# A hybrid SSD / retention / RWKV-7 decoder trunk with a routed mixture of experts: the routing of tokens to experts is rearranged

## The chip, the core and the metric

The kernel runs on one core of one Trainium2 chip. Its engines work side by side: TensorE (PE in the profile; PEld is its loading of the stationary operand), VectorE (DVE), ScalarE (ACT), GpSimd (POOL) and SyncE (SP, which here only starts transfers). The metric is the device time of the whole program in microseconds.

## The reference

Two layers over 512 tokens of width 1024, all float32. Layer 0 mixes tokens by SSD and retention with one output projection; layer 1 by RWKV-7 time mixing. Each layer ends in the mixture of experts that this change is about:

```
def hier_moe(h, wg, bg, we, be, w1, w3, w2):
    g_logits = t @ wg + bg                       # 4 groups
    g_prob = softmax(g_logits); g_idx = argmax(g_logits); g_gate = g_prob[g_idx]
    e_logits = (t @ we + be).reshape(-1, 4, 4)   # 16 experts
    top_v, top_i = top_k(e_logits[g_idx], 2)
    top_w = softmax(top_v) * g_gate
    combine = sum(one_hot(g_idx * 4 + top_i, 16) * top_w)
    for e in range(16):
        he = silu(t @ w1[e]) * (t @ w3[e])
        out = out + combine[:, e] * (he @ w2[e])
...
for layer in range(2):
    h = h + mix(rms_norm(h, norm_mix_w[layer]))
    h = h + hier_moe(rms_norm(h, norm_ffn_w[layer]), ...)
return rms_norm(h, norm_final_w)
```

## The kernel before

The program is a row of phases with a barrier between them. A phase is one block in which each engine has its own instruction stream; the streams meet by semaphores written out by hand (`wait_ge`, `then_inc`), and every engine works strictly in the order of its code. Nothing is scheduled by a planner, so what stands ahead of an instruction in its stream can hold it.

**Ahead of the experts.** Layer 0 ends its mixer in `proj_phase`, layer 1 in `rwkv_out_phase`. Both multiply by an output matrix, one tile of 128 tokens (m = 0 to 3) after another, add to the residual `t.h`, and run the RMSNorm `Norm` on it: `mean_square`, `root`, `inverse`, `scale` (into `xn`), `transposes` on TensorE into PSUM banks, `evacuate` into `ut`, the transposed tokens. `norm.store` writes `xn` to `token_rows` in HBM, from where tokens are gathered. In `rwkv_out_phase` the products of tile m use the banks 4 to 7, and so do the norm's transposes of tile m - 1.

**Routing.** `moe` starts with the logits (TensorE, in bands, then folded), the choice of group and two experts (`first_max`, three times, on VectorE), and counts: each token gets its rank in its expert's list by products with triangular and all-one matrices (`s_rank`). A list is cut into LARGE pieces of 96 slots and SMALL pieces of 64. VectorE works out which expert each visit serves (`listed`, written to `t.meta`, from where every engine reads it into a register by `expert` and `visits`) and at which slot it begins (`begins`).

**Visits.** The loop over visits treats two pieces at a time: A (96 tokens of expert e = 0's list, buffers `xa`) and B (64 tokens, `xb`). To find the tokens of a piece, VectorE compares the ranks with slot numbers (`equal_slots`), multiplies by token numbers (`times_ids`), sums (`sum_a`, `sum_b`); TensorE turns the result into a column (`turn_a`, `turn_b`); VectorE writes it as row numbers (`index_a`, `index_b`); GpSimd gathers the rows (`gather_b` one transfer, `gather_a` two); TensorE transposes them (`x_transposes`); VectorE evacuates (`x_evacuation`). Only then can the visit's products start (`s_xte`). A visit's products: with `w13` in four chunks j (release: `s_used`, `s_h`), SiLU and gating, transposes, then with `w2` in two chunks (release: `s_half`, `s_y`). SP loads the next visit's weights into each chunk as it is released: for two experts 8 transfers of 1 MB for `w13` and 4 for `w2`, 12.6 MB a visit.

Before the loop, the kernel gathers the tokens of visit 0 **and** of visit 1; inside visit i it finds and gathers those of visit i + 2, behind the first half of the `w2` products. SP loads the weights of expert 0 and then those of the first A piece at the start of `moe`, and waits for the whole table (`s_meta` at 3) before it enters its loop.

Of the kernel before, what the change touches and what calls it, by code (L numbers as in the profile page):

```python
# [21 lines left out]
P = 128  # L22
# [22 lines left out]
LARGE_UNITS = -(-(SEQ - SMALL) // LARGE)  # L45
# [6 lines left out]
ROUTER_ROWS = 32  # L52

# [25 lines left out]
def shape_constants():  # L79
# [9 lines left out]
    iota4 = np.tile(np.arange(4), (P, 1))  # L89
# [3 lines left out]
    more = np.tile((head[:, None] + LARGE * np.arange(LARGE_UNITS)[None, :] + SMALL).reshape(1, -1), (P, 1))  # L93
# [5 lines left out]
    common = np.concatenate([ident, upto, before, neg, same_half, half_sel, iota4, visit, np.ones((P, P)), fold, slot_of, row_of, iota16, np.tile(head, (P, 1)), more, expert_step, row_half], 1).astype(f)  # L99
# [17 lines left out]
C_IOTA = C_HALF + 2  # L117
C_VISIT = C_IOTA + 4
# [7 lines left out]
C_EXPERT_STEP = C_MORE + EXPERTS * LARGE_UNITS  # L126
C_ROWHALF = C_EXPERT_STEP + UNIT_LISTS
C_ALL = C_ROWHALF + STEPS
# [56 lines left out]

class Norm:
# [39 lines left out]
    def transposes(self, pe, m):  # L226
        t = self.t
        pe.wait_ge(self.s_xn, m + 1)
        if self.used[m] is not None:
            pe.wait_ge(self.s_ev, 2 * (self.used[m] + 1))  # L230
        for k in range(KD):
            mm = t.nc.tensor.transpose(t.bank[self.banks[m][k // 4]][:, (k % 4) * P:(k % 4 + 1) * P], self.xn[:, m, k * P:(k + 1) * P], t.ident)  # L232
            if k % 4 == 3:
                mm.then_inc(self.s_tr, 1)

# [87 lines left out]
def load_phase(t, a):  # L323

    nc = t.nc
    with ExitStack() as c:
# [13 lines left out]
        def _(act):  # L340
# [4 lines left out]
            act.dma_start(t.router[:, :, :, :], a["router"]).then_inc(t.s_more, 16)  # L345
# [8 lines left out]
def in_proj_phase(t, a, ut, xbc, xc, z, g, v, q, k, dt, bt, qr, kr, qt, kt, kd, tmp, a_dt, nacum, cum, ecum, ea):  # L354
# [26 lines left out]
    with ExitStack() as c:  # L381
# [23 lines left out]
        def _(pe):  # L405
            for i, (kind, n, m) in enumerate(steps):
# [464 lines left out]
def proj_phase(t, tag, srcs, scales, mt, chunks, ring, w_sem, ffn_layer):  # L871
# [5 lines left out]
    with ExitStack() as c:  # L877
# [11 lines left out]
        def _(sp):  # L889
            for n in range(2, len(chunks)):  # L890
# [5 lines left out]
                sp.dma_start(ring[n % 2], chunks[n]).then_inc(w_sem[n % 2], 16)  # L896
            norm.store(sp, ffn_layer)

        @block.tensor
        def _(pe):  # L900
# [7 lines left out]
            for n in range(len(chunks)):  # L908
                half, part = divmod(n, n_half)
                pe.wait_ge(w_sem[n % 2], 16 * (n // 2 + 1))  # L910
                for m in range(NT):
# [8 lines left out]
                    if n == len(chunks) - 1 and m:  # L920
                        norm.transposes(pe, m - 1)
            norm.transposes(pe, NT - 1)

# [12 lines left out]
        def _(dve):  # L936
            for half in range(2):
# [8 lines left out]
            for m in range(NT):  # L946
                norm.evacuate(dve, m)
# [13 lines left out]
def ffn_norm(t, c, layer, banks, used):  # L961

    A = views(t, AT_FFN, [("ut", (KD, SEQ)), ("xn", (NT, D))])
# [4 lines left out]
def moe(t, a, layer):  # L968

    nc = t.nc  # L970
    NL = GROUPS + EXPERTS
# [9 lines left out]
                     ("table", (2, TABLE, UNIT_LISTS))])  # L981
    ut, bank = A["ut"], t.bank
    w13, w2 = (a[n][layer] for n in ("moe_w13", "moe_w2"))
    w_col = t.col(f"ffn{layer}")
    with ExitStack() as c:
        sem = lambda n: t.semaphore(f"moe{layer}_{n}")
        s_part, s_lg, s_exp, s_route, s_pick, s_prefix, s_rank = (sem(n) for n in (
            "partial_logits", "logits", "exp", "route", "picked", "prefixes", "ranked"))
# [4 lines left out]
        s_w13 = [sem(f"w13_loaded{i}") for i in range(4)]  # L993
        s_w2 = [sem(f"w2_loaded{i}") for i in range(2)]
# [4 lines left out]
        taken = [AT_FFN + KD * SEQ + NT * D]  # L999
# [7 lines left out]
        wr = t.router[:, layer]  # L1007
        lg = sb("logits", [P, NT, NL])
        oh_g, cand_g = (sb(n, [P, NT, GROUPS]) for n in ("group", "cand_g"))
        sel, cand = (sb(n, [P, NT, EXPERTS]) for n in ("sel", "cand"))  # L1010
        mx = [sb(f"max{j}", [P, NT]) for j in range(3)]
        least, ex, den, gsum = (sb(n, [P, NT]) for n in ("least", "ex", "den", "gsum"))
# [3 lines left out]
        parts = sb("parts", [P, SEQ])  # L1016
        prod, over = (sb(n, [P, NT, EXPERTS]) for n in ("prod", "over"))
        in_head = sb("in_head", [P, NT])
        more = sb("more", [P, EXPERTS, LARGE_UNITS])
        units, begin, incl = (sb(n, [P, UNIT_LISTS]) for n in ("units", "begin", "incl"))  # L1020
# [8 lines left out]
        match_a, match_b = sb("match_a", [P, LARGE, NT]), sb("match_b", [P, SMALL, NT])  # L1029
        token_a, token_b = sb("token_a", [P, LARGE]), sb("token_b", [P, SMALL])  # L1030
        scaled = sb("scaled", [P, 2, TABLE, UNIT_LISTS])
# [17 lines left out]
        def _(sp):  # L1049
            for j in range(4):  # L1050
                sp.dma_start(b["w13"][:, 1, 2 * j:2 * j + 2], w13[0, j]).then_inc(s_w13[j], 16)
            for j in range(2):
                sp.dma_start(b["w2"][:, 1, 2 * j:2 * j + 2], w2[0, j]).then_inc(s_w2[j], 16)
            n = visits(sp)
            first = expert(sp, 0, 0)
            for j in range(4):
                sp.dma_start(b["w13"][:, 0, 2 * j:2 * j + 2], w13[bass.ds(first, 1), j].rearrange("o p k n -> p (o k) n")).then_inc(s_w13[j], 16)
            for j in range(2):
                sp.dma_start(b["w2"][:, 0, 2 * j:2 * j + 2], w2[bass.ds(first, 1), j].rearrange("o p k n -> p (o k) n")).then_inc(s_w2[j], 16)
            sp.wait_ge(s_meta, 3)  # L1060
# [21 lines left out]
        def _(pe):  # L1082
            quarters = P // ROUTER_ROWS
            for k in range(KD):
                r0 = k % quarters * ROUTER_ROWS
                mm = nc.tensor.matmul(bank[0][r0:r0 + ROUTER_ROWS, :], wr[:, k, :], ut[:, k, :],
                                      start=k < quarters, stop=k >= KD - quarters)
            mm.then_inc(s_part, 1)
            pe.wait_ge(s_part, 2)
            for m in range(NT):  # L1090
                mm = nc.tensor.matmul(bank[2][:, m * NL:(m + 1) * NL], parts[:, m * P:(m + 1) * P], t.common[:, C_FOLD:C_FOLD + NL],
# [1550 lines left out]
```

## Time and profile before

| what | value |
|---|---|
| median of 3 runs | 1708.24 us (1707.78 to 1712.01) |
| the profiled execution | 1702.24 us, its span 1700.4 us |
| TensorE busy | 1478.2 us, 87% of the span |
| VectorE / ScalarE / GpSimd busy | 37% / 22% / 11% |
| granted TensorE clock, mean | 0.94 of full |
| read from HBM / written | 304.64 MB / 27.26 MB |

The times of all rows below are counted from the start of the span. Layer 0's projection phase ends at 566.9, its loop over visits runs from 601.0 to about 853; layer 1's experts begin at 1377.2, their loop at 1411.6.

### The profile page before, as it was taken

To read this page: it belongs to the slowest core of one execution; us is meant where nothing else is said; L and a number is where in the kernel's file an instruction comes from. 1 tells how busy PE (TensorE), PEld (TensorE's weight loads), DVE (VectorE), ACT (ScalarE), POOL (GpSimd) and SP (SyncE) were. 2 spreads that over 40 slices of the span, in tenths; PEclk is the share of its full clock that TensorE was granted. 3 is DMA by queue.
4 is the path that set the end of the run, shared out by engine and by line. 5 is a ranking of instruction groups with operands and counts; after the bars stand their busy time and mean duration, and the time that the engine had idled before them with its cause. 6 is when DMAs were issued, how large, how long until landed. Compare 5 with 4: busy or idle time off the path is not lost. (4 is left out here: it accounts for less than half of the span.)

```text
span 1700.4 us, 26012 instructions
## 1 busy us (share of the span) xinstructions
PE 1478.2 (87%) x10560; PEld 759.3 (45%) x10560; DVE 623.5 (37%) x1271; ACT 375.6 (22%) x706; POOL 192.7 (11%) x211
## 2 busy tenths in 40 slices
PE   6999999979799489988929999989998858999891
PEld 3444444457444233333314444458996423343330
DVE  4421200048101542211247269455667244131124
ACT  1012111133200111111144067242232110111112
POOL 0000000016000010100020024110131001010002
PEclk9999999989899689999969999998999968999996
DMA  5424321020020699999852211000011059999995
GB/s 186 148 99 168 129 99 50 0 99 1 1 99 25 253 368 415 417 414 418 356 175 103 99 50 50 25 1 3 27 51 51 37 209 365 411 417 412 417 399 191
DMA packets 73060, 307.72 MB, mean 181 GB/s; under 512 B 7584, under 2 KB 9760, under 8 KB 48032
## 3 DMA queue, kind: packets, MB, share of 16 engines
q1 hardware_dynamic: 54736, 262.68, 39.1%
q0 software_dynamic: 9344, 31.99, 5.0%
q10 hardware_dynamic: 8912, 12.10, 2.0%
q8 instruction: 48, 0.79, 0.2%
q14 instruction: 20, 0.16, 0.0%
HBM read 304.64 MB, written 27.26 MB: 195 GB/s over the span
## 5 line engine op out<-in xcount | busy, mean ns | idle before, releaser
L1149 PE MATMUL bank<-arena 128*32 128x512 f32 x2048 | 241.2, 613 | 25.3 <-DMA arena<-in_moe_w 24.1
L446 PE MATMUL bank<-arena 128*128 128x512 f32 x512 | 222.1, 592 | 0.0
L1569 PE MATMUL bank<-arena 128*128 128x512 f32 (+1 forms) x448 | 192.7, 601 | 1.4 <-ACT arena L1672 1.4
L446 PEld LDWEIGHTS bank<-arena 128*128 128x128 f32 x512 | 96.3, 190 | 117.5 <-issue 117.5
L1434 DVE TENSOR_TENSOR arena<-arena,bank 64x512 f32<-64x512 f32 x32 | 22.1, 691 | 332.4 <-ACT arena L1215 332.4
L1465 POOL DMA_INDIRECT arena<-token_rows,index x60 | 56.9, 948 | 730.4 <-DVE index L1298 694.6
L1149 PEld LDWEIGHTS bank<-arena 128*32 128x32 f32 x2048 | 65.6, 113 | 164.1 <-issue 124.1
L1569 PEld LDWEIGHTS bank<-arena 128*128 128x128 f32 (+1 forms) x448 | 83.4, 191 | 103.0 <-issue 97.9
L1181 PE MATMUL bank<-arena 128*32 128x512 f32 x1024 | 116.5, 595 | 0.0
L913 PE MATMUL bank<-arena 128*128 128x512 f32 x256 | 110.5, 593 | 1.5 <-ACT arena L929 1.5
L443 PE MATMUL bank<-arena 128*128 128x512 f32 x192 | 82.6, 592 | 1.2 <-PEq L275 1.2
L913 PEld LDWEIGHTS bank<-arena 128*128 128x128 f32 x256 | 48.4, 190 | 61.5 <-issue 59.8
L1215 ACT ACTIVATE arena<-bank 64x512 f32<-64x512 f32 x32 | 18.8, 588 | 236.2 <-PE bank L1149 236.2
L1156 PE MATMUL bank<-arena 128*32 128x256 f32 x1024 | 66.9, 379 | 0.0
L2353 PE MATMUL bank<-arena 128*128 128x512 f32 x128 | 57.5, 609 | 5.4 <-DVE arena L239 5.4
L232 PE MATMUL bank<-common,arena 128*128 128x128 f32 x128 | 23.1, 349 | 43.9 <-ACT arena L218 40.0
L471 ACT ACTIVATE arena<-bank 128x512 f32<-128x512 f32 x32 | 19.1, 597 | 189.4 <-PE bank L446 189.4
L443 PEld LDWEIGHTS bank<-arena 128*128 128x128 f32 x192 | 36.4, 190 | 46.9 <-issue 45.4
L1181 PEld LDWEIGHTS bank<-arena 128*32 128x32 f32 x1024 | 30.0, 109 | 58.8 <-issue 57.4
L1156 PEld LDWEIGHTS bank<-arena 128*32 128x32 f32 x1024 | 32.9, 110 | 50.2 <-issue 39.0
L2225 DVE TENSOR_TENSOR arena<-bank,common 128x512 f32<-128x512 f32 x48 | 31.0, 687 | 60.6 <-PE bank L2008 60.5
L941 DVE TENSOR_TENSOR h<-h,bank 128x512 f32<-128x512 f32 x8 | 5.5, 688 | 114.0 <-PE bank L913 114.0
(373 smaller groups left out, 1916.4 us busy)
## 6 DMA issues: line engine op xcount, KB each, us to landing
arena<-in_moe_w SPq DMA_DIRECT2D x216, 1024.0 KB
arena<-in_w_in_e SPq DMA_DIRECT2D x11, 2048.0 KB, 9.1
slot_rows<-zero POOLq DMA_DIRECT2D x20, 512.0 KB, 7.9
arena<-in_w_out_e SPq DMA_DIRECT2D x4, 2048.0 KB, 8.6
slot_rows<-arena ACTq DMA_DIRECT2D x64, 128.0 KB, 8.1
token_rows<-arena SPq DMA_DIRECT2D x8, 512.0 KB, 2.6
arena<-in_rw_wr SPq DMA_DIRECT2D x2, 2048.0 KB, 12.9
arena<-in_rw_wk SPq DMA_DIRECT2D x2, 2048.0 KB, 7.9
```

The costliest lines, as they stand in the source:

```text
L232: mm = t.nc.tensor.transpose(t.bank[self.banks[m][k // 4]][:, (k % 4) * P:(k % 4 + 1) * P], self.xn[:, m, k * P:(k + 1) * P], t.ident)
L443: mm = nc.tensor.matmul(bank[:, :], w[:, kk, m * P:(m + 1) * P], ut[:, kk, :], start=kk == 0, stop=kk == KD - 1)
L446: mm = nc.tensor.matmul(bank[:, 0:width], ut[:, kk, m * P:(m + 1) * P], w[:, kk, 0:width], start=kk == 0, stop=kk == KD - 1)
L913: mm = nc.tensor.matmul(t.bank[4 * half + m][:, :], mt[:, part * KD + kk, m * P:(m + 1) * P], ring[n % 2][:, kk, :], start=part == 0 and k ...
L1149: mm = nc.tensor.matmul(bank[H[s]][band * BAND:(band + 1) * BAND, :], xt[:, kk, half, s * BAND:(s + 1) * BAND], b["w13"][:, e, k, w * FF:( ...
L1156: mm = nc.tensor.matmul(bank[H[2]][band * BAND:(band + 1) * BAND, 0:FF // 2], b["xta"][:, kk, half, SMALL:LARGE], b["w13"][:, 0, k, band * ...
L1181: mm = nc.tensor.matmul(bank[Y[s]][band * BAND:(band + 1) * BAND, :], b["ht"][:, k, s * PAIR + e * BAND:s * PAIR + (e + 1) * BAND], b["w2" ...
L1434: nc.vector.tensor_tensor(u, b["silu"][PAIR:P, s, :], bank[H[s]][PAIR:P, :], ALU.mult).then_inc(s_u, 1)
L1465: return nc.gpsimd.indirect_dma_start(out=x, out_offset=None, in_=halves, in_offset=bass.IndirectOffsetOnAxis(ap=t.index[0:n, at:at + 1], ...
L1569: mm = nc.tensor.matmul(t.bank[i % BANKS][0:rows, :], left, right, start=n == 0, stop=n == len(pairs) - 1)
L2225: nc.vector.tensor_tensor(four(u[name][rr]), four(t.bank[5 + (f + rr) % 3][:, :]), mask(col), ALU.mult).then_inc(s_sc_e, 1)
L2353: mm = nc.tensor.matmul(t.bank[4 + 2 * (m % 2) + half][:, :], mt[:, k_, m * P:(m + 1) * P], ring[half][:, k_, :], start=k_ == 0, stop=k_ = ...
```

## The change

1. **Logits.** Each `Norm.logits(m)` multiplies the tokens of a tile by the router's 20 columns (8 products) inside the phase ahead of `moe`, into bank 5. `proj_phase` evacuates each tile's transposes as it goes instead of all at the end.
2. **Loads of expert 0** (`FirstExpert.load`, six transfers of 1 MB) are issued by SP in the phase ahead, before `norm.store`: in `proj_phase` after the seventh product group, in `rwkv_out_phase` after the RWKV norm of the last tile.
3. **Choice by counting rivals.** The logits lie in a padded array with -3e38 around each group of four. Every logit is compared with its three rivals on the left (>=) and on the right (>); the sum is its place in the group. Place 0 is the first, place below 2 is among the two.
4. **New lists.** Large and small pieces of each expert are counted in one comparison of 192 elements. A visits beyond the large pieces take small pieces from the end of the list. The first A expert is worked out ahead of everything else and handed to SP alone (`s_meta` at 1).
5. **First rows by products.** The tokens of visit 0's A piece are no longer gathered: TensorE multiplies `xn` by the selection matrix `match_a` (`first_x`, two halves of 16 products).
6. **One gather less ahead.** Before the loop only visit 0 is prepared. Inside visit i the tokens of visit i + 1 are turned behind the first `w13` chunk, indexed, gathered, and transposed in the same visit.
7. **Softmax and expert weights** move on VectorE from the choice to behind the last evacuation before the loop. SP now waits for `s_meta` at 4 before its loop.
8. **RWKV's last norm in other banks.** In `rwkv_out_phase` the norm's transposes use the banks 0 to 3, and products of tile m wait for the residual add of tile m - 2 only.

```
+class FirstExpert:
+    def load(self, sp):
+        for j in range(4):
+            sp.dma_start(self.room13[:, 1, 2 * j:2 * j + 2], self.w13[0, j]).then_inc(self.s_w13[j], 16)
+        for j in range(2):
+            sp.dma_start(self.room2[:, 1, 2 * j:2 * j + 2], self.w2[0, j]).then_inc(self.s_w2[j], 16)
+    def logits(self, pe, layer, m):
+        pe.wait_ge(self.s_ev, 2 * m + 2)
+        for k in range(KD):
+            t.nc.tensor.matmul(t.bank[LOGITS][:, m * ROUTED:(m + 1) * ROUTED], self.ut[:, k, m * P:(m + 1) * P], t.router[:, layer, k, 0:ROUTED],
...
 # rwkv_out_phase, tensor
-                    pe.wait_ge(norm.s_ev, 2 * (m - 1))
+                    pe.wait_ge(s_add, 2 * (m - 1))
...
-                if m:
-                    norm.transposes(pe, m - 1)
                 if m + 2 < NT:
                     transposes(m + 2)
+                if m:
+                    pe.wait_ge(s_ev, 2 * min(m + 2, NT))
+                    norm.transposes(pe, m - 1)
...
 # moe, tensor: before the loop
+            pe.wait_ge(s_matched, 1)
+            first_x(0)
             pe.wait_ge(s_tokens_b, 1)
             turn_b()
+            first_x(1)
             pe.wait_ge(s_xb, 16)
             x_transposes(b["xb"], 1, P)
...
 # moe, tensor: in the loop
+                    if j == 0:
+                        pe.wait_ge(s_tokens_b, i + 2)
+                        turn_b()
+                        pe.wait_ge(s_tokens_a, i + 1)
+                        turn_a()
...
 # moe, vector: before the loop
+            ch.add(nc.vector.tensor_tensor(beats[:, :, :, 0:3], rivals(0), alone, ALU.is_ge))
+            ch.link(nc.vector.tensor_tensor(beats[:, :, :, 3:6], rivals(EPG), alone, ALU.is_gt))
+            ch.link(nc.vector.tensor_reduce(place[:, :, :].rearrange("p m e -> p (m e)"), beaten[:, :, :], AX.X, ALU.add))
...
+            dve.wait_ge(s_xt, 1)
+            x_evacuation(b["xtb"], 1, 0, P)
+            dve.wait_ge(s_meta, 3)
+            second = [expert(dve, e, 1) for e in range(2)]
...
             listed(2, TABLE)
             nc.vector.tensor_copy(meta_of[:, :, 2:TABLE], of_visit[0:1, :, 2:TABLE]).then_inc(s_meta, 1)
             begins(2, TABLE)
...
 # moe, vector: in the loop
                 both = [expert(dve, e, i + 2) for e in range(2)]
+                dve.wait_ge(s_turned_b, i + 2)
+                dve.wait_ge(s_xb, 16 * i + 16)
+                index_b()
+                dve.wait_ge(s_turned_a, i + 1)
+                index_a()
                 for s in range(2):
                     dve.wait_ge(s_silu, STEPS * i + s + 1)
```

TensorE's order around the end of layer 0's projection and the start of routing. Before (L913 output products, L232 the norm's transposes, L1086 and L1091 logits, L1097 to L1100 ranks, L1105 to L1114 turns, L1120 transposes of gathered rows):

```order
L913 MATMUL bank<-arena 128x512 x8
L232 MATMUL bank<-common,arena 128x128 x16
L877 UNCONDITIONAL_BRANCH
L1081 UNCONDITIONAL_BRANCH
L1086 MATMUL bank<-arena,router 32x512 x8
L1091 MATMUL bank<-common,arena 128x20 x4
L1097 MATMUL bank<-arena,common 128x64
L1099 MATMUL bank<-arena,common 128x48
L1100 MATMUL bank<-arena,common 128x16
```

In the changed kernel (L941 products, L251 transposes, L259 logits, L1120 to L1124 ranks, L1151 `first_x`, L1129 `turn_b`, L1144 transposes of `xb`):

```order
L941 MATMUL bank<-arena 128x512 x8
L251 MATMUL bank<-common,arena 128x128 x8
L259 MATMUL bank<-narrow,arena 128x20 x16
L251 MATMUL bank<-common,arena 128x128 x8
L259 MATMUL bank<-narrow,arena 128x20 x16
L903 UNCONDITIONAL_BRANCH
L1116 UNCONDITIONAL_BRANCH
L1120 MATMUL bank<-arena,common 128x64
...
L1151 MATMUL bank<-arena 128x96 x16
L1129 MATMUL bank<-common,arena 64x1 x2
L1151 MATMUL bank<-arena 128x96 x16
L1144 MATMUL bank<-common,arena 128x128 x4
```

The logits moved ahead of the phase's end, 16 products among the last transposes and 16 behind them, and 32 products of 96 columns stand between the ranks and the loop.

VectorE's order at the entry of the loop over visits. Before (L1425 is the last weight of the experts, L1041 and L1046 load registers, L1434 and L1436 the gating, L1302 evacuates transposed rows; the indices follow at the end of the visit):

```order
L1425 TENSOR_TENSOR weight<-weight,arena 128x4
L1041 TENSOR_LOAD meta
L1041 ISA x2
L1429 UNCONDITIONAL_BRANCH
L1429 ISA
...
L1434 TENSOR_TENSOR arena<-arena,bank 64x512
...
L1436 TENSOR_TENSOR arena<-arena,bank 64x256
```

In the changed kernel (L1452 is that last weight; L1318 and L1314 are `index_b` and `index_a`; L1466 and L1468 the gating):

```order
L1452 TENSOR_TENSOR weight<-weight,arena 128x4
L1079 TENSOR_LOAD meta
L1079 ISA x2
L1456 UNCONDITIONAL_BRANCH
...
L1318 TENSOR_TENSOR index<-bank,common 128x1
L1461 REGISTER_ALU
L1314 TENSOR_TENSOR index<-bank,common 128x1
L1314 TENSOR_TENSOR index<-bank,common 64x1
...
L1466 TENSOR_TENSOR arena<-arena,bank 64x512
```

The row numbers of visit 1 are now written after the whole table, the slots and the weights of the experts, and ahead of visit 0's gating; before, both pieces of visit 1 were indexed ahead of the table.

## Rows read from the trace of the kernel before

**Rows 1.** Page, costliest groups: line, engine, tiles xcount | busy, mean ns | idle, releaser

```profile
L1149 PE MATMUL bank<-arena 128*32 128x512 f32 x2048 | 241.2, 613 | 25.3 <-DMA arena<-in_moe_w 24.1
```

**Rows 2.** Windows: stretch, engines' busy us (instructions), granted clock, DMA share, GB/s

```profile
600.00:605.00 5.00, 4.40 (x24) 1.25 (x27) 4.90 (x7) 0.00 (x0) 2.82 (x3) 0.51 1.01 413
...
720.00:740.00 20.00, 17.37 (x192) 5.90 (x188) 0.69 (x1) 2.64 (x4) 0.34 (x1) 1.00 1.02 412
```

**Rows 3.** Timeline of TensorE in layer 0's loop: start, us, line [idle <-releaser]

```profile
601.01 5.53 PE L1149 MATMUL bank<-arena 128*32 128x512 f32 x32 [0.60 <-DVE arena L1302]
...
632.20 3.62 PE L1149 MATMUL bank<-arena 128*32 128x512 f32 x32
...
661.47 3.62 PE L1149 MATMUL bank<-arena 128*32 128x512 f32 x32
...
763.82 3.64 PE L1149 MATMUL bank<-arena 128*32 128x512 f32 x32 [2.71 <-DMA arena<-in_moe_w]
```

**Rows 4.** Timeline of SP's weight loads, both layers

```profile
607.89 13.65 SPq L1070 DMA_DIRECT2D arena<-in_moe_w  x8
...
627.64 5.97 SPq L1078 DMA_DIRECT2D arena<-in_moe_w  x4
...
1419.35 13.66 SPq L1070 DMA_DIRECT2D arena<-in_moe_w  x8
```

**Rows 5.** Timeline, end of layer 0's projection and routing, and layer 1's logits

```profile
551.89 7.03 PE L913 MATMUL bank<-arena 128*128 128x512 f32 x16
...
571.31 1.07 PE L1091 MATMUL bank<-common,arena 128*128 128x20 f32 x8 [0.71 <-ACT arena L1203]
...
572.42 0.24 DVE L1249 TENSOR_TENSOR arena<-bank,rows 128x80 f32<-128x80 f32 x1 [5.33 <-PE bank L1091]
...
579.52 0.27 DVE L1323 SCALAR_TENSOR_TENSOR arena<-bank,arena 128x64 f32<-128x64 f32 x1 [1.13 <-PE bank L1100]
...
1381.62 1.89 PE L1091 MATMUL bank<-common,arena 128*128 128x20 f32 x8 [0.71 <-ACT arena L1203]
```

**Rows 6.** Timeline of the gathers before layer 0's loop

```profile
584.86 1.02 POOL L1465 DMA_INDIRECT arena<-token_rows,index  x1 [163.40 <-DVE index L1298]
...
590.99 1.19 POOL L1465 DMA_INDIRECT arena<-token_rows,index  x1 [0.30 <-issue]
...
591.53 1.11 PE L1120 MATMUL bank<-common,arena 128*128 128x128 f32 x4 [2.60 <-DMA arena<-token_rows,index]
...
598.68 1.73 PE L1120 MATMUL bank<-common,arena 128*128 128x128 f32 x8 [5.30 <-DMA arena<-token_rows,index]
```

**Rows 7.** The gathers' source line L1465: time from issue to landing

```profile
DMA to landing us min/median/max: 3.2/8.0/9.6
```

**Rows 8.** Timeline of VectorE and TensorE in layer 0's visit 0

```profile
600.79 1.25 DVE L1310 TENSOR_TENSOR arena<-arena 128x1056 f32<-128x1056 f32 x1
...
604.66 0.17 DVE L1392 CAST meta<-arena 1x32 int32<-1x32 f32 x1
...
612.74 0.17 DVE L1425 TENSOR_TENSOR weight<-weight,arena 128x4 f32<-128x4 f32 x1
...
622.85 3.64 PE L1181 MATMUL bank<-arena 128*32 128x512 f32 x32
...
623.54 0.35 DVE L1444 TENSOR_SCALAR arena<-arena 128x4 f32 x2
...
626.25 0.41 DVE L1290 TENSOR_REDUCE arena<-arena 128x64 f32<-128x256 f32 x1
```

**Rows 9.** Source line L1046: loading a register on VectorE, ns min/median/max

```profile
L1046 DVEq TENSOR_LOAD <-meta x38: 300/307/547, 585.2 to 1628.1; - x38
...
L1046 DVEq FUSED_REGOPS  x54: 71/190/216, 585.8 to 1628.5; - x54
```

**Rows 10.** Timeline of TensorE at the end of rwkv_out_phase

```profile
1337.72 15.67 PE L2353 MATMUL bank<-arena 128*128 128x512 f32 x32 [2.39 <-DVE arena L239]
...
1357.24 13.97 PE L2353 MATMUL bank<-arena 128*128 128x512 f32 x32 [2.98 <-DVE arena L239]
```

More of the change, by code:

```diff
@@ L98, in shape_constants @@
     fold = np.tile(np.eye(ROUTER_ROWS, GROUPS + EXPERTS), (P // ROUTER_ROWS, 1))
-    common = np.concatenate([ident, upto, before, neg, same_half, half_sel, iota4, visit, np.ones((P, P)), fold, slot_of, row_of, iota16, np.tile(head, (P, 1)), more, expert_step, row_half], 1).astype(f)
+    common = np.concatenate([ident, upto, before, neg, same_half, half_sel, visit, np.ones((P, P)), fold, slot_of, row_of, iota16, np.tile(head, (P, 1)), more, expert_step, row_half, -2 * visit - 1], 1).astype(f)
     lg = np.log(1.0 - 2.0 ** (-5.0 - np.arange(R_HEADS)))
@@ L921, in _ @@
                         norm.transposes(pe, m - 1)
+            norm.logits(pe, ffn_layer, 0)
+            norm.logits(pe, ffn_layer, 1)
             norm.transposes(pe, NT - 1)
+            norm.logits(pe, ffn_layer, 2)
+            norm.logits(pe, ffn_layer, 3)
         @block.scalar
@@ L945, in _ @@
                         norm.inverse(dve, m)
[L946 to L947 removed]
+                        if m:
+                            norm.evacuate(dve, m - 1)
+            norm.evacuate(dve, NT - 1)
 def first_max(nc, chain, onehot, x, mx, least, cand, iota):
@@ L1005, in sb @@
             return v
[L1007 to L1010, printed above, removed]
+        lists = ROUTED // EPG
+        beaten = sb("beaten", [P, NT * lists * EPG, 6])
+        place = sb("place", [P, NT, lists * EPG])
+        oh_g = sb("group", [P, NT, GROUPS])
         mx = [sb(f"max{j}", [P, NT]) for j in range(3)]
-        least, ex, den, gsum = (sb(n, [P, NT]) for n in ("least", "ex", "den", "gsum"))
+        ex, den, gsum = (sb(n, [P, NT]) for n in ("ex", "den", "gsum"))
         gexp = sb("gexp", [P, NT, GROUPS])
@@ L1082, in _ @@
         def _(pe):
[L1083 to L1091, printed above, removed]
-                                      start=True, stop=True)
-            mm.then_inc(s_lg, 1)
             flat = lambda ap: ap.rearrange("p m e -> p (m e)")
@@ L2311, in _, with rwkv_out_phase @@
             normed.squares(pool, 2)
-def rwkv_out_phase(t, a, y, v, g, lnw, lnb, sq, mt, ring, s_w, keep):
+def rwkv_out_phase(t, a, y, v, g, lnw, lnb, sq, mt, ring, s_w, keep, first):
     nc = t.nc
@@ L2326, in _ @@
         def _(sp):
+            sp.wait_ge(normed.s_y, 1)
+            first.load(sp)
             norm.store(sp, 1)
@@ L2443, in rwkv @@
     rwkv_scan_phase(t, a, M["sigma"], M["ag"], M["r"], M["k"], V["v"], V["g"], btok, ktok, u, state, keep, wo_ring, s_w)
-    rwkv_out_phase(t, a, btok, V["v"], V["g"], u["lnw"], u["lnb"], u["sq"], M["r"], wo_ring, s_w, keep)
+    first = FirstExpert(t, a, 1)
+    rwkv_out_phase(t, a, btok, V["v"], V["g"], u["lnw"], u["lnb"], u["sq"], M["r"], wo_ring, s_w, keep, first)
+    return first
 def final_phase(t, a, out, w, rows, y):
```

333 lines of the change are left out of this document (165 added, 168 removed).

## The prediction, made before the changed kernel was run

> **What bounds the kernel now.** I read the page's costliest groups first. They say who waits in the long loops over visits: TensorE's largest group idles 25.3 us in all, 24.1 of them for weights [rows 1]. The windows show why: in the middle of the loop the DMA share is 1.02 at 412 GB/s, TensorE is busy 17.37 of 20 us [rows 2]. Two paces stand against each other. Visits 1 and 2 start 29.3 us apart with no wait (632.20 and 661.47) [rows 3]. A visit's 12.6 MB of weights, its gathers (0.66 MB) and its stores (0.64 MB) take 13.9 MB / 412 GB/s = 33.7 us. So TensorE lives on weights loaded ahead and starves once these are used up [rows 3]. From there each layer ends when SP's stream of loads ends: only what moves that stream, or tears a hole into it, moves the end. The chain of waits covers only the last 27 us and tells nothing about routing.
>
> Next I read SP's timeline. The stream starts at 607.89 in layer 0 and at 1419.35 in layer 1; layer 0's first `w2` loads follow at 627.64 [rows 4]. Eight `w13` loads are 8.4 MB = 20.4 us. With 1 us from issue to first bytes (my choice), the `w13` part flows until 629.3, so the `w2` loads were there in time and the stream has no hole. In layer 1 the same point is 1440.7.
>
> **The change part by part, layer 0.** *Start of routing.* The last products end at 558.9 (551.89 + 7.03) [rows 5]. Then TensorE has 8 transposes, 16 products of 20 columns for the logits of two tiles, 8 transposes, 16 + 16 products again. Two instructions a product, 8 in 1.07 us at full clock (0.134 each) [rows 5], transposes at the same: 1.1 + 4.3 + 1.1 + 4.3 = 10.8, and 0.35 for the barrier: the logits are there at 570.0, before at 572.42 [rows 5]. The evacuations hide under the logits of earlier tiles.
>
> *Choice, ranks.* Before: 7.1 us from logits to ranks (572.42 to 579.52) [rows 5]. Now seven VectorE steps: 80 elements 0.24, three of 240 at 0.41 as for 256 elements [rows 8], two of them overlapping, two small at 0.2, gaps of 0.04: 1.9. Three prefix adds and two products: 1.7. Ranks at 573.6. Nine short steps give the first A expert (2.2) and six more its selection matrix (1.7): 577.5.
>
> *`first_x`.* No row shows it. Each half is 16 products, 32 instructions, bound by loading 128 x 128 operands as the logits are: 0.134 each at full clock, 0.236 at the low one (8 in 1.89) [rows 5], so 4.3 to 7.6 us. TensorE has idled by then, and in this stage the clock stood at 0.51 (1.2 GHz) until TensorE had worked for some microseconds [rows 2]. I take 6.7 for the first half: 584.2. `turn_b` and `index_b` 0.6, GpSimd starts 0.9 later: 585.7, before 584.86 [rows 6]. The B gather landed 6.7 us after GpSimd's start (591.53 - 584.86) [rows 6]: 592.4. The second half of `first_x` ends by 592.2 even at the low clock, hidden by that gather; without this cover it would cost its 4.3 to 7.6. Transposes and evacuation take 1.8 (2.1 for two pieces, 598.68 to 600.79) [rows 6, 8]. Call this point E: 594.2, before 600.79. The loop starts 6.6 us earlier.
>
> The Trainium skill (TensorE: Matmul & The Clock Gate, "Part 1: The HAM clock gate") says that throttled is the default state and activity releases it; it speaks against moving row selection onto an idle TensorE, and the rows at 0.51 agree. By it alone both halves could run low, which would move E by 0.9 us.
>
> *What VectorE has to do after E.* Two register loads at 0.55 (0.307, plus 0.19 of register arithmetic) [rows 9]: 1.1. Finding visit 1's pieces: 3.1 (623.54 to 626.66) [rows 8]. The softmax part moved here, ten short steps: 1.9. The table up to its cast to integers: 4.0 (600.79 to 604.83) [rows 8]. The rest, slots and weights: 8.1 (to 612.91) [rows 8]. Loop entry with three register loads: 2.0. Together 20.2 us. Only then does VectorE write visit 1's row numbers, though the tokens were turned long before. Queued behind them are visit 0's gating and GpSimd's gathers.
>
> *Visit 0's hole.* GpSimd starts 0.9 after the index, its third transfer 2.5 later (0.95 to 1.19 each and 0.30 between), landing 7.7 after that as in 590.99 to 598.68 [rows 6]: E + 31.3. The last transposes and the `ht2` evacuation: 2.0. The first half of `w2` up to SP's issue: 4.8 (622.85 to 627.64) [rows 4, 8], and 1.5 more since TensorE idled over 5 us and restarts at the low clock. SP issues visit 1's `w2` at E + 39.6 = 633.8; bytes flow from 634.8. SP waits for the table too, so its `w13` loads start at E + 1.1 + 3.1 + 1.9 + 4.0 + 1.5 (entry) = 605.8 and flow until 627.2. So the stream has a hole of 7.6 us and resumes 5.5 us later than before (634.8 against 629.3). Visit 1 then starts near 638 where it was 632.20 [rows 3], still with enough loaded ahead. Traffic behind that point is the same seven gathers and stores. **Layer 0: +5.5.**
>
> A gather's landing decides here. The Trainium skill (DMA: Bandwidth & Descriptors, "Anatomy of one DMA — SWDGE (gpsimd) path") puts a transfer at a fixed 2 us plus its bytes over 436 GB/s, an estimate of 2.6 us for 0.26 MB; with it the hole would shrink by 5 us and E come 4 earlier. The median of this line is 8.0 [rows 7], with the DMA engines full of weights, and I keep 7.7.
>
> **Layer 1.** In `rwkv_out_phase` TensorE waited 2.39 and 2.98 us for the norm's evacuations of the shared banks, and after the first wait a tile's products took 15.67 instead of 13.97 [rows 10]. The other banks take all three away: 7.1 us. The products end at 1357.24 + 13.97 - 7.1 = 1364.1. From there the steps are those of layer 0 (E came 35.3 after the products' end): E = 1399.4, bytes of `w2` from 1399.4 + 40.6 = 1440.0, before 1440.7. **Layer 1: -0.7.**
>
> **The rest.** Expert 0's loads move 16 us forward in layer 0, more in layer 1, where the DMA engines are nearly idle: worth nothing, as weights were not what E waited for; `norm.store` waits some 3 us behind them on SP and its rows are needed only at 585.7. In each layer's last visit a useless gather of 0.66 MB (1.6 us of DMA) no longer competes with the last stores: -0.5 each, between 0 and -1.6. Inside later visits the gathers start after the first chunk and have 15 us before TensorE asks: nothing. Contiguous router columns, constants: nothing.
>
> **Sum.** +5.5 - 0.7 - 1.0 = +3.8 on the profiled 1702.24. The runs shown have a median 6.0 above it, so I forecast 1708.24 + 3.8 = 1712.0 us.
>
> **Rivals.**
> *Faster: the hole does not open.* Should rows of visit 1 arrive by E + 24 (the `w13` loads flow until E + 33), SP's start is what counts: E + 11.6, so 605.8 for 607.89 and 1411.0 for 1419.35: -2.1 and -8.3, with the tails -11.4, 1697. It needs gathers 7 us faster than [rows 6]; the least landing, 3.2, speaks for it, the median against. With half of that, about 1704. Chance 0.24. Were the skill's 2.6 us a gather right, the time would be about this rival's; with no landing of the trace below 3.2 I give that 0.03 of the 0.24.
> *Slower: gathers land late under a full SP queue.* Both gathers on the path at the longest landing, 9.6 [rows 7]: 2.9 on E and 1.9 on visit 0, 4.8 a layer, +9.6 more: 1721.6. From about 0.7 us over my price a layer it decides for slower. For it: visit 0's gather meets SP's backlog, the old ones before the loop met less. Chance 0.36.
> *No change that can be told:* the 6.6 us won before the loop are given back in the hole and layer 1's bank gain pays for the rest; my sum is there. Chance 0.40.
>
> **Range and chances.** Per layer `first_x` is open by -2.4 to +0.9, the two landings by -7 to +4.8 at their ends, the restart clock by 1.5, register loads by 1. Two layers together give about -11 to +9: 1701 to 1721, 1712 likeliest. What a measurement tells from no change is 0.3%, 5.1 us. Faster 0.24, within 0.40, slower 0.36.
>
> **What would show it.** Right: ranks near 573.6, `first_x` 4 to 8 us a half, the loop near 594 and 1399; VectorE's first index in the loop some 20 us later, TensorE idle ahead of visit 0's transposes for the gather, a dip of the DMA share around 627 to 634, the next visit near 638; no waits of TensorE on evacuations in `rwkv_out_phase`. Wrong: transposes of visit 0 without a wait, or DMA at 1.0 throughout.

## The result, and the profile after

The changed kernel took 1720.4 us (median of four runs, 1718.2 to 1723.1), the kernel before 1708.0 on the same chip: a ratio of 1.0076 with a 95% interval of 1.0064 to 1.0088. It is slower, by 0.8% or 12 us. I had forecast 1712.0 with a range of 1701 to 1721 and a chance of 0.36 for slower. The profiled execution spans 1717.4 us, 17.0 more than that of before; some 4 us of these 17 are, as argued below, not the change's.

The page's rows that answer to [rows 1] and [rows 10], line, engine, tiles and count | busy, mean ns | idle, releaser:

```profile
L1173 PE MATMUL bank<-arena 128*32 128x512 f32 x2048 | 243.0, 616 | 29.1 <-DMA arena<-in_moe_w 27.3
...
L2375 PE MATMUL bank<-arena 128*128 128x512 f32 x128 | 55.6, 592 | 0.0
```

TensorE's wait for weights grew by 3.2 us and the waits of the RWKV output phase are gone. The page can't say more; the stretch around routing can. Timeline of the changed kernel, TensorE and VectorE, end of layer 0's projection phase to visit 1:

```profile
560.17 4.00 PE L259 MATMUL bank<-narrow,arena 128*128 128x20 f32 x32
...
564.01 1.95 PE L251 MATMUL bank<-common,arena 128*128 128x128 f32 x8
...
565.75 6.85 PE L259 MATMUL bank<-narrow,arena 128*128 128x20 f32 x32
...
572.90 0.25 DVE L1278 TENSOR_TENSOR arena<-bank,rows 128x80 f32<-128x80 f32 x1 [6.21 <-PEq L903]
...
577.04 0.36 DVE L1343 TENSOR_TENSOR arena<-bank,common 128x192 f32<-128x192 f32 x1 [1.35 <-PE bank L1124]
...
598.51 6.47 PE L1173 MATMUL bank<-arena 128*32 128x512 f32 x32 [0.87 <-DVE arena L1322]
...
619.17 0.16 DVE L1318 TENSOR_TENSOR index<-bank,common 128x1 uint32<-128x1 f32 x1 [2.43 <-issue]
...
627.51 1.11 PE L1144 MATMUL bank<-common,arena 128*128 128x128 f32 x4 [5.87 <-DMA arena<-token_rows,index]
...
631.22 1.73 PE L1144 MATMUL bank<-common,arena 128*128 128x128 f32 x8 [2.60 <-DMA arena<-token_rows,index]
...
642.63 3.61 PE L1173 MATMUL bank<-arena 128*32 128x512 f32 x32
```

Read from the end. Visit 1 starts at 642.63 (before 632.20 [rows 3]). Before it TensorE waited 5.87 and 2.60 us for the gathers of visit 1's rows, whose row numbers VectorE wrote only at 619.17. The loop itself starts at 598.51, earlier than the 601.01 of [rows 3], but far less than the 6.6 us I had counted on. SP's loads (both layers) and the windows over the same stretch:

```profile
611.08 9.42 SPq L1105 DMA_DIRECT2D arena<-in_moe_w  x8
638.81 5.24 SPq L1113 DMA_DIRECT2D arena<-in_moe_w  x4
...
1428.99 8.72 SPq L1105 DMA_DIRECT2D arena<-in_moe_w  x8
1457.34 5.22 SPq L1113 DMA_DIRECT2D arena<-in_moe_w  x4
```

```profile
560.00:565.00 5.00, 5.00 (x41) 5.00 (x39) 2.77 (x6) 1.44 (x2) 0.00 (x0) 0.83 1.02 429
565.00:570.00 5.00, 5.00 (x26) 5.00 (x24) 1.38 (x2) 0.00 (x0) 0.00 (x0) 0.50 0.96 342
...
630.00:635.00 5.00, 3.78 (x22) 2.02 (x26) 2.56 (x7) 0.28 (x1) 0.00 (x0) 0.50 0.96 387
635.00:640.00 5.00, 5.00 (x60) 1.56 (x52) 1.96 (x4) 0.00 (x0) 0.00 (x0) 1.00 0.09 20
640.00:645.00 5.00, 5.00 (x60) 1.68 (x56) 0.00 (x0) 1.58 (x3) 0.00 (x0) 1.00 0.93 372
...
1160.00:1170.00 10.00, 8.22 (x95) 7.63 (x94) 1.29 (x2) 1.68 (x3) 0.00 (x0) 0.53 0.01 2
1170.00:1180.00 10.00, 10.00 (x85) 9.21 (x85) 3.44 (x5) 2.00 (x4) 0.00 (x0) 0.50 0.01 2
...
1450.00:1455.00 5.00, 5.00 (x31) 1.75 (x34) 4.51 (x10) 0.28 (x1) 0.00 (x0) 0.58 0.55 229
1455.00:1460.00 5.00, 5.00 (x60) 1.68 (x56) 0.00 (x0) 0.60 (x1) 0.00 (x0) 1.00 0.32 90
```

The DMA share of 0.09 at 635 to 640 is the hole in the stream of weights. By the prediction's sum the `w13` loads issued at 611.08 have flowed by 632.5 (20.4 us and 1 to the first bytes), and the `w2` loads issued at 638.81 bring bytes from 639.8: 7.3 us. That sum leaves out visit 1's gathers, 0.66 MB or 1.6 us of the same DMA engines; by the shares the engines themselves were idle for some 5 us (0.96, 0.09 and 0.93 in the three windows from 630). Layer 1 has the same hole, by the sum between 1450.4 and 1458.3, by the shares of 0.55 and 0.32 some 5.7 us idle.

Along the program the profiled execution falls behind like this: 10.4 us at layer 0's visit 1 and 11.2 at its end; 14.9 where the RWKV output phase starts; 8.7 at its last product; 17.5 at layer 1's visit 1; 17.0 at the end. The 3.7 us between the second and the third figure lie in code that the change leaves alone: the granted clock was 0.53 and 0.50 from 1160 to 1180. The kernel before had 0.77 and 1.00 there, and the same code had 0.50 and 0.84 in run 1 and 0.67 and 1.00 in run 3. The timed medians stand 12.4 apart, not 17.0. So I take this stretch for the spread of single executions. Without it layer 0 costs 11.2 us, the output phase gives 6.2 back, layer 1's routing costs 8.8 to its visit 1, and 0.5 come back to the end: 13.3 in all.

### The profile page after: what moved, and what is told of

It is laid out like the page before. It is cut to its first block and busy times, and to the rows that moved or that the text cites. A ratio compares the mean times of both kernels' runs of the same rounds, so it can differ in the third digit from the quotient of the medians.

```text
span 1717.4 us, 26254 instructions
## 1 busy us (share of the span) xinstructions
PE 1508.8 (88%) x10700; PEld 799.2 (47%) x10700; DVE 632.3 (37%) x1261; ACT 374.4 (22%) x704; POOL 182.0 (11%) x201
## 5 line engine op out<-in xcount | busy, mean ns | idle before, releaser
L1173 PE MATMUL bank<-arena 128*32 128x512 f32 x2048 | 243.0, 616 | 29.1 <-DMA arena<-in_moe_w 27.3
L1173 PEld LDWEIGHTS bank<-arena 128*32 128x32 f32 x2048 | 67.6, 113 | 163.2 <-issue 124.1
L1491 POOL DMA_INDIRECT arena<-token_rows,index x50 | 47.0, 939 | 701.1 <-DVE index L1314 442.2
L1210 PE MATMUL bank<-arena 128*32 128x512 f32 x1024 | 118.6, 604 | 0.0
L941 PE MATMUL bank<-arena 128*128 128x512 f32 x256 | 110.5, 593 | 1.7 <-ACT arena L961 1.7
L1466 DVE TENSOR_TENSOR arena<-arena,bank 64x512 f32<-64x512 f32 x32 | 22.1, 690 | 201.6 <-ACT arena L1237 201.5
L941 PEld LDWEIGHTS bank<-arena 128*128 128x128 f32 x256 | 48.4, 190 | 61.8 <-issue 59.8
L1210 PEld LDWEIGHTS bank<-arena 128*32 128x32 f32 x1024 | 31.8, 111 | 63.7 <-issue 59.7
L1180 PEld LDWEIGHTS bank<-arena 128*32 128x32 f32 x1024 | 34.6, 110 | 48.3 <-issue 38.0
L1318 DVE TENSOR_TENSOR index<-bank,common 128x1 uint32<-128x1 f32 x18 | 2.9, 159 | 146.2 <-PE bank L1129 141.4
L251 PE MATMUL bank<-common,arena 128*128 128x128 f32 x128 | 22.8, 346 | 37.0 <-ACT arena L237 37.0
```

What stands on the lines that cost most here:

```text
L941: mm = nc.tensor.matmul(t.bank[4 * half + m][:, :], mt[:, part * KD + kk, m * P:(m + 1) * P], ring[n % 2][:, kk, :], start=part == 0 and k ...
L1173: mm = nc.tensor.matmul(bank[H[s]][band * BAND:(band + 1) * BAND, :], xt[:, kk, half, s * BAND:(s + 1) * BAND], b["w13"][:, e, k, w * FF:( ...
L1180: mm = nc.tensor.matmul(bank[H[2]][band * BAND:(band + 1) * BAND, 0:FF // 2], b["xta"][:, kk, half, SMALL:LARGE], b["w13"][:, 0, k, band * ...
L1210: mm = nc.tensor.matmul(bank[Y[s]][band * BAND:(band + 1) * BAND, :], b["ht"][:, k, s * PAIR + e * BAND:s * PAIR + (e + 1) * BAND], b["w2" ...
L1466: nc.vector.tensor_tensor(u, b["silu"][PAIR:P, s, :], bank[H[s]][PAIR:P, :], ALU.mult).then_inc(s_u, 1)
L1491: return nc.gpsimd.indirect_dma_start(out=x, out_offset=None, in_=halves, in_offset=bass.IndirectOffsetOnAxis(ap=t.index[0:n, at:at + 1], ...
```

## The experiments

Ratios are to the kernel before on the same chip; differences between two kernels are those of the ratios times 1708 us. My theory, **the hole**: visit 1's row numbers stand behind the table, slots and weights on VectorE, hence late gathers, late `w2`, and idle DMA. Rivals: SP's later start, gathers held up by the full DMA queue, the low clock.

### 1. Row numbers early

```
             nc.vector.tensor_copy(meta_of[:, :, 2:TABLE], ...).then_inc(s_meta, 1)
+            dve.wait_ge(s_turned_b, 2); dve.wait_ge(s_xb, 16); index_b()
+            dve.wait_ge(s_turned_a, 1); index_a()
...
-                (the same five lines at the head of the loop's body)
+                (at its end, for visit i + 2; TensorE turns once more behind the loop)
```

> The changed kernel, but VectorE writes visit 1's row numbers as soon as the table's cast is out (near 608.7 us in layer 0) and no longer behind slots and weights (619.17); in the loop it writes each next visit's numbers at the end of the body. Theory of the hole: GpSimd starts near 609.7, the third gather's issue is near 612.3 and lands 8.6 us later, near 621, about when TensorE gets there; w2 starts near 625, SP issues visit 1's w2 near 629.5, ahead of 632.5 where its w13 loads (issued from 611.08) have flowed. The dips of the DMA share near 635 to 640 in layer 0 and 1450 to 1459 in layer 1 vanish: -7.3 and -7.9 us, so 1705 us where the changed kernel has 1720.4. Rival, SP's late start (611.08 for 607.89) is what costs: no change, 1720. Rival, gathers meet the full DMA queue: half the gain, 1713.

Measured: 1703.3 us, ratio 0.9984 (0.9973 to 0.9995): 15.7 us below the changed kernel. GpSimd and TensorE in layer 0:

```profile
611.57 0.91 POOL L1500 DMA_INDIRECT arena<-token_rows,index  x1 [0.30 <-issue]
...
619.81 0.65 PE L1190 MATMUL bank<-common,arena 128*128 128x128 f32 x4 [1.60 <-DVE arena L1470]
620.30 1.43 PE L1144 MATMUL bank<-common,arena 128*128 128x128 f32 x12
...
630.40 3.62 PE L1173 MATMUL bank<-arena 128*32 128x512 f32 x32
```

The last gather is issued at 611.57, and the twelve transposes run at 620.30 without a wait. Visit 1 starts 12.2 us earlier. The edit moves the row numbers in later visits too, but there it changes nothing: the next gather starts 5.8 us behind the start of visit 1 in this kernel (636.20) and in the changed one (648.41). This one position in VectorE's order is worth more than all that the change costs.

### 2. SP starts early

```
-            sp.wait_ge(s_meta, 4)
+            sp.wait_ge(s_meta, 3)
             with sp.Fori(0, n) as i:
...
+                sp.wait_ge(s_meta, 4)          # last in the loop's body
```

> The changed kernel, but SP waits only for visit 1's experts ahead of its first loads of the loop, and for the rest of the table at the end of the loop's first pass; the w13 loads then start when TensorE is through its first chunk, near 607 for 611.08. Theory of the hole: the stream resumes where w2 is issued, and that hangs on the late row numbers; the hole only grows by what comes earlier: 1720 plus or minus 1.5 us. Rival, SP's start is what counts: -4 us a layer, 1712.

Measured: 1719.3 us, ratio 1.0080 (1.0063 to 1.0096), no change that can be told.

```profile
607.42 14.19 SPq L1105 DMA_DIRECT2D arena<-in_moe_w  x8
639.72 5.24 SPq L1113 DMA_DIRECT2D arena<-in_moe_w  x4
```

The stream started 3.7 us earlier and resumed no earlier: SP's start is not what costs while the hole is open. That rival falls.

### 3. Both

The two edits above, with the row numbers written even ahead of `listed(2, TABLE)`.

> Both edits, with visit 1's row numbers written even ahead of the long table. Theory of the hole: once rows are early the stream's start counts too: -7.6 and about -2.5 a layer, 1700 us, and faster than the kernel before (1708). Rival, only the row numbers count: as the first of these kernels, 1705. Rival, neither: 1720.

Measured: 1697.8 us, ratio 0.9958 (0.9945 to 0.9971): 20 us below the changed kernel, and below the kernel before. That is 4.4 us more than the first run. Two things differ from it, SP's start and the still earlier row numbers; in the first run the transposes already found their rows without a wait, while SP's loads start at 603.57 here for 610.16 there. So I put the gain down to SP's start, which counts once the hole is nearly shut. TensorE and the windows:

```profile
619.66 0.66 PE L1191 MATMUL bank<-common,arena 128*128 128x128 f32 x4 [3.15 <-DVE arena L1471]
```

```profile
625.00:630.00 5.00, 5.00 (x60) 1.60 (x56) 1.37 (x3) 0.47 (x1) 0.00 (x0) 1.00 0.74 252
```

What is late next is the gating of visit 0 (L1471), which stands behind slots and weights on VectorE; the share of 0.74 is what is left of the hole.

### 4. The banks alone

On the kernel before; the order of the two transposes is changed as in the diff ahead of the prediction:

```
-        norm = ffn_norm(t, c, 1, [(4 + 2 * (m % 2), 5 + 2 * (m % 2)) for m in range(NT)], (None,) * NT)
+        norm = ffn_norm(t, c, 1, [(2 * (m % 2), 1 + 2 * (m % 2)) for m in range(NT)], (None, None, 0, 1))
...
-                    pe.wait_ge(norm.s_ev, 2 * (m - 1))
+                    pe.wait_ge(s_add, 2 * (m - 1))
```

> The kernel before with only the RWKV norm's banks and the order around them changed. As I priced it: three waits gone, -7.1 us of 1708, so 1701. By the trace of the changed kernel (the phase took 61.8 us from its first transposes to its last product, before 67.8): -6.0, so 1702. Rival, the time is given back where layer 1's weights or routing wait anyway: 1708.

Measured: 1698.2 us, ratio 0.9964 (0.9949 to 0.9978), -6.1 us. Its products run without a wait and each tile at 13.90:

```profile
1338.96 13.90 PE L2353 MATMUL bank<-arena 128*128 128x512 f32 x32
...
1353.57 13.90 PE L2353 MATMUL bank<-arena 128*128 128x512 f32 x32
```

It isn't given back. If the two parts add up, routing as changed costs some 19 us, from which the banks take 6.

### 5. Logits among wide products

```
                     if n == len(chunks) - 1 and m:
                         norm.transposes(pe, m - 1)
+                    if n == len(chunks) - 1 and m >= 2:
+                        norm.logits(pe, ffn_layer, m - 2)
-            norm.logits(pe, ffn_layer, 0)
-            norm.logits(pe, ffn_layer, 1)
```

> The changed kernel, but in layer 0's projection phase the logits of tiles 0 and 1 stand between the wide products of tiles 2 and 3 and not behind the last of them. The work on TensorE is the same. Theory of the clock: the granted clock fell from 1.00 to 0.50 while TensorE was busy without a gap, behind 4 us of 20-column products; with half of them among wide products the transposes of tile 3 take 1.04 for 1.95 us and most of the last logits 0.125 each for 0.21: the choice starts 2 to 4 us earlier, and all of layer 0 with it: -3 of 1720.4, so 1717.4. Rival, the clock falls as early or the same time is lost elsewhere: 1720.

Measured: 1720.4 us, ratio 1.0066 (1.0050 to 1.0082), not told from the changed kernel; the expected 3 us aren't excluded by the times either. The trace decides:

```profile
563.22 1.86 PE L259 MATMUL bank<-narrow,arena 128*128 128x20 f32 x16
566.26 1.09 PE L251 MATMUL bank<-common,arena 128*128 128x128 f32 x8 [1.18 <-ACT arena L237]
567.19 6.21 PE L259 MATMUL bank<-narrow,arena 128*128 128x20 f32 x32
...
573.70 0.24 DVE L1278 TENSOR_TENSOR arena<-bank,rows 128x80 f32<-128x80 f32 x1 [5.46 <-PEq L903]
```

This execution was 1.25 us late before the edit could act (tile 1's transposes at 552.82 for 551.56), which has to be taken off. The transposes of tile 3 were at full clock, as I expected, but came 1.0 us later: the products of tile 3, and the norm that hangs on them, stood behind the moved logits. The last logits lost the clock all the same (6.21 for 6.85). The choice started at 573.70 for 572.90, so with the 1.25 taken off only 0.45 us earlier where I expected 2 to 4. The expectation was wrong: the last tile's norm is the chain here.

### 6. A dose

```
+            for _ in range(4):
+                ch.link(nc.vector.tensor_tensor(scaled[:, :, 2:TABLE, :], (itself), (itself), ALU.mult))
             dve.wait_ge(s_meta, 4)
             n = visits(dve)
```

> The changed kernel with four extra VectorE products of 1,056 elements (some 5.2 us) ahead of its loop, whose results nothing reads: a dose. Theory of the hole: visit 1's row numbers are 5.2 us later, TensorE waits as much longer, and since nothing else ends last there every us counts: +5.2 a layer, 1731. Rival, gathers are held up by the full DMA queue and land when the w13 loads let them: less than half, 1723. Rival, the hole costs nothing: 1720.

Measured: 1729.4 us, ratio 1.0124 (1.0107 to 1.0140), 8.2 us above the changed kernel. That is four fifths of the 10.4 added, and far from the rival's "less than half". In the traces visit 1 starts 4.6 us later in layer 0 (647.23 for 642.63), and layer 1's `w2` loads are issued 9.3 us later (1466.64 for 1457.34). The last gather took less time to TensorE's transposes than in the changed kernel, 7.8 us (626.92 to 634.69) and not 8.6 (622.66 to 631.22): some tenths of the dose are won back there.

### 7. Expert 0's loads late

```
             (first.load(sp) taken out of both preceding phases)
+            first.load(sp)
             sp.wait_ge(s_meta, 1)
             first_a = expert(sp, 0, 0)
```

> The changed kernel with expert 0's six loads back at the start of the routing phase, in both layers. As I priced their move: nothing, 1720 plus or minus 2. Rival: now they flow while the B gather is under way, which lands some us later (its 7.4 us from GpSimd's start to TensorE's transposes), and E with it: +2 to +4 a layer, 1724 to 1728. Rival: the token rows' stores no longer stand behind them on SP, a gain: 1718.

Measured: 1720.7 us, ratio 1.0070 (1.0057 to 1.0083). The loads were issued at 574.08 for 551.75, and the transposes of the B gather ran at 597.28 for 596.52, in an execution that was 1.1 us late before the edit could act; from GpSimd's start they took 7.0 us for 7.4. The early loads are worth nothing that can be measured, as I had priced them.

### 8. Slots and weights last

```
-            (slots and weights, from spare to t.weight[:, :, 1], ahead of the loop)
+            ch.wait()
             dve.wait_ge(s_meta, 4)
             n = visits(dve)
             with dve.Fori(0, n) as i:
...
+            (the same lines behind the loop)
```

> The kernel with both edits (early row numbers, SP's early start), and besides slots and weights moved from ahead of VectorE's loop to behind it. In the kernel with both edits TensorE waits 3.15 us for VectorE's gating of visit 0, which stands behind that block, and the DMA share still dips to 0.74 between 625 and 630. Theory: the wait goes, w2 starts near 619 for 622.5 and the dip closes: -3 a layer, 1692 where it had 1697.8. Rival: the dip was the gathers' and stays, 1697. Rival: the block behind the loop delays the combination: above 1698.

Measured: 1692.9 us, ratio 0.9907 (0.9893 to 0.9921): 16 us below the kernel before, 29 below the changed one. TensorE, VectorE and the windows:

```profile
619.15 0.66 PE L1191 MATMUL bank<-common,arena 128*128 128x128 f32 x4 [0.57 <-DVE arena L1440]
...
854.13 0.15 DVE L1466 TENSOR_SCALAR arena<-arena 128x1 f32<-128x1 f32 x1
...
859.26 0.16 DVE L1496 TENSOR_TENSOR weight<-weight,arena 128x4 f32<-128x4 f32 x1
...
866.40 1.28 DVE L292 SCALAR_TENSOR_TENSOR h<-arena,weight,h 128x1024 f32<-128x1024 f32 x1 [6.98 <-DMA arena<-slot_rows,slot]
```

```profile
625.00:630.00 5.00, 5.00 (x64) 1.95 (x60) 0.41 (x1) 1.21 (x3) 0.00 (x0) 1.00 1.01 419
```

That is 8.7 us below run 3 by the ratios, where 6 were expected. The wait of 3.15 is down to 0.57, the share is 1.01 where it was 0.74, and the 5.3 us of slots and weights hide behind the last visit.

### 9 to 12. TensorE kept busy

```
+            def keep_busy(n):
+                for _ in range(n):
+                    nc.tensor.matmul(bank[Y[2]][:, 0:256], ones, t.common[:, 0:256], start=True, stop=True)
...
             first_x(1)
+            keep_busy(9)
             pe.wait_ge(s_xb, 16)
```

The second kernel adds `keep_busy(2)` ahead of the ranks and `keep_busy(4)` ahead of `first_x(0)`.

> The kernel with slots behind the loop (1692.9), and TensorE kept busy while it waits for the first B gather: nine products of 256 columns of constants into an unused bank, which nothing reads, some 4 us at full clock. There the granted clock was 0.50 and the first chunk of visit 0 took 6.28 us in layer 0 and 5.07 in layer 1, where 3.62 is its time at full clock. Theory of the clock: the chunk takes 3.6 to 4, SP's first w13 loads of the loop start as much earlier, and with them both streams: -2.6 and -1.4, so 1689. Rival, the products outlast the gather or take something from it: 1693 or more. Rival, the hole reopens since TensorE now reaches visit 0's transposes earlier: 1693.

> As the kernel before it, with two such products more ahead of the ranks and four between ranks and the selection matrix, so that the first half of the row selection by products runs at the full clock: 3.81 us, as its second half does, for 6.54 and 7.00. The rows of visit 0 come 2.7 and 3.2 us earlier, and the loop with them: -10 in all, 1683. Rival: TensorE in these stretches is too little busy even so, the clock stays at 0.50 and the products only delay the ranks: 1690 to 1694.

Measured: 1689.6 us, ratio 0.9913 (0.9899 to 0.9927), and for the second 1686.9 us, 0.9895 (0.9868 to 0.9921). On this chip the kernel before took 1705.1, so only the ratios compare: times 1708 they are 1693 and 1690, the values of the rivals. The first kernel's timeline, layers 0 and 1:

```profile
596.05 3.64 PE L1179 MATMUL bank<-arena 128*32 128x512 f32 x32 [0.86 <-DVE arena L1332]
...
1399.56 3.64 PE L1179 MATMUL bank<-arena 128*32 128x512 f32 x32 [0.86 <-DVE arena L1332]
```

The chunk takes 3.64 us, as expected, yet the ratio can't be told from run 8's. In the second kernel the first half of the row selection still took 5.88 us for the 3.81 expected, with the granted clock at 0.60 from 580 to 585: the added products didn't lift it there. Run 12 below has none of them there and took 5.90 at 0.58. I ran kernels 8 and 9 again on one chip:

> The kernel with slots behind the loop once more, on the same chip as the next one: on two chips their ratios to the kernel before were 0.9907 and 0.9913, each known to 0.0014, while the traces differ by 7 us. If the trace is right this one is at 0.991 and the next 0.002 to 0.004 below it.

> TensorE kept busy while it waits for the B gather, once more. Theory of the clock: the loop starts 2 us earlier and its first chunk takes 3.64 us for 6.28, so 3 to 7 us below its neighbour on the same chip. Rival: what the trace showed was the spread of single executions, and the two stand within 1.5 us.

Measured: 1691.4 us, ratio 0.9903 (0.9886 to 0.9920), and 1690.4 us, 0.9900 (0.9882 to 0.9917). The traces say that the loop's first `w13` loads go out 2.6 us earlier (601.10 for 603.72) and that layer 0's last visit reaches its last chunk 2.3 us earlier (832.10 for 834.36), layer 1's 4.4. Part of that is lost again in the same chunks; run 11 first, then run 12, each with layers 0 and 1:

```profile
834.36 3.64 PE L1174 MATMUL bank<-arena 128*32 128x512 f32 x32 [1.93 <-DMA arena<-in_moe_w]
...
1640.55 3.64 PE L1174 MATMUL bank<-arena 128*32 128x512 f32 x32 [2.70 <-DMA arena<-in_moe_w]
```

```profile
832.10 5.34 PE L1179 MATMUL bank<-arena 128*32 128x512 f32 x32 [2.08 <-DMA arena<-in_moe_w]
...
1399.27 5.34 PE L1179 MATMUL bank<-arena 128*32 128x512 f32 x32 [0.86 <-DVE arena L1332]
...
1636.16 4.97 PE L1179 MATMUL bank<-arena 128*32 128x512 f32 x32 [2.94 <-DMA arena<-in_moe_w]
```

Behind waits of 2 to 3 us for weights a chunk took 3.64 us at one place and about 5.3 at another in both kernels (in run 11 5.34 at 767.68 and at 801.45), so nothing ties it to the edit. Run 12's last visits therefore end only 0.6 and 3.0 us earlier (transposes behind the chunk at 838.88 for 839.43, 1642.58 for 1645.62). And in run 12 the added products kept the clock in layer 0 only: in layer 1 TensorE still idled 1.98 us for the gather and the first chunk took 5.34. The times are 1 us apart. Whether keeping the clock is worth anything in time stays open; anything near 7 us is out.

## Why the prediction was right, and where it fell short, point by point

The mechanism was the one described, and the range held the time, but by 0.6 us and with luck: what moved the time most, a low clock while TensorE is busy, isn't among the terms the range was made of. The likeliest case, no change that can be told, did not come about, and the forecast of 1712.0 is 8 us short. The step that failed is the start of routing.

**What bounds the kernel** (only what moves SP's stream or tears a hole into it moves the end) held: runs 1, 2 and 6 moved the time by -15.7, +0.7 and +8.2 as the theory says.

**Start of routing: mis-sized.** I priced 32 instructions of logits at 0.134 each and had them done at 570.0; the choice began at 572.90, no earlier than before. The phase ran 0.5 us late, the transposes of tile 3 took 1.95 instead of 1.1, and the last logits 6.85 instead of 4.3 (0.21 each): 3.4 us at the low clock, of which the quicker first logits gave some back. The step failed in "at full clock". I had looked for a low clock only where TensorE had idled.

**Choice, ranks.** 4.1 us for 3.6: the count over a stride (128x80 from 128x480) takes 0.65, and I had 0.41.

**`first_x`.** 6.7 us predicted, 6.70 measured; the second half (3.81) was hidden by the B gather. That gather took 7.4 us to TensorE's transposes for 6.7. In sum E came at 598.4, not 594.2: 2.4 us before the old one instead of 6.6. Of the 4.2 us missing, 2.9 are the start of routing, 0.5 choice and ranks, 0.7 the gather. They, and 0.8 more behind E, make layer 0 +10.4 instead of +5.5.

**What VectorE has to do after E.** 20.2 us predicted, 20.8 measured (598.4 to 619.17).

**Visit 0's hole.** All relative to E: gathers in at +31.3 (measured +32.8), SP's `w2` issue at +39.6 (measured +40.4), hole 7.6 us (7.3 by the same sum). The mechanism and the size by that sum were right; its origin was 4.2 us late, and SP's first loads came 1.1 later still (E + 12.7, predicted E + 11.6). The sum itself isn't what the DMA engines show: they were idle for some 5 us, since the gathers took their share behind the `w13` loads. My sum left that out. A gather's price, taken from [rows 6] against the 2.6 us of the Trainium skill (DMA: Bandwidth & Descriptors, "Anatomy of one DMA — SWDGE (gpsimd) path"), held in the main: the last gather took 8.6 us to TensorE's start, 0.9 more than my 7.7. The landing times of the gathers' source line run from 6.8 to 9.3 us: the trace disagrees with the page's figure here, where the DMA engines are full of weights.

**Layer 1.** The output phase gave 6.2 us back for 7.1 predicted (6.1 in run 4). E came 37.1 us after the products' end, I had 35.3, by the same low clock. The `w2` bytes came 2.7 us later than before on that layer's own scale, where I had 0.7 earlier.

**The rest.** Expert 0's early loads: nothing, as predicted (run 7). The tails, -0.5 each in the sum, were -0.4 in layer 0, from the start of the last products to the last residual add (27.3 us before, 26.9 after), and -1.2 in layer 1, to the end of the span (36.2 and 35.0).

**The rivals.** "Slower" came about, but not by its mechanism: I had it from gathers at 9.6 us, and it came for the most part from a low clock ahead of E; the two gathers on the path were only 0.7 and 0.9 us over my price. "Faster, the hole does not open" was built in run 1, where it gave 1703; with SP's start as well, 1698, for the 1697 that I had worked out. That these two agree is in part chance: E is late there too, and SP starts earlier than the rival had it (603.57 for 605.8).

## What to carry to other kernels

When work is moved out of one critical stretch, list what each engine's in-order queue then holds ahead of the next transfer's trigger: here three short index instructions behind some 10 us of slots, weights and loop entry cost 15.7 us, more than the whole change costs in sum (run 1). Put the trigger first and whatever only the end needs last (run 8, with SP's early start in it, against the changed kernel: 29 us). A stream of transfers with a hole in it can hide a gain ahead of the hole (run 2), so close the hole before judging such a gain. Price narrow products at both clocks.

## What the hardware showed unexpectedly

The granted clock fell from 1.00 to 0.50, from 2.4 to 1.2 GHz, while TensorE was busy for 5.00 of every 5 us. The mean of 0.83 from 560 to 565 puts the fall at about 563.3. Since 559.30 it had done 128 x 128 transposes and 20-column products, whose weight loads filled the time (PEld 5.00 of 5). The Trainium skill (TensorE: Matmul & The Clock Gate, "Part 1: The HAM clock gate") ties the throttled state to idle time and the released one to activity; by that section these products would have run at the full clock. The rows disagree: TensorE was busy and the clock fell. These products cost 0.125 us an instruction before the fall and 0.21 after it. Run 5 showed the fall again behind the same kind of work. Which of the two kinds of instruction it hangs on was not tested.

Two reduces took longer for the same elements in the changed layout of the selection matrices, in which they step over their input: 128x96 from 128x384 took 0.81 us for 0.55 before, 128x64 from 128x256 took 0.60 for 0.41 [rows 8]. The comparisons ahead of them, over the same arrays, took 0.89 us for two in both kernels. That the stride is the cause is argued from the code; no run tested it.
